# Moving the row factor of six RMS norms from the inputs of the products to their outputs, with the small vectors in three transfers and the first stage's rotation done by DVE from PSUM

## The chip, the cores and the metric

The kernel runs on one core of one Trainium2 chip. The metric is the device time of one execution, in microseconds. Engines are named as in the profile: PE multiplies matrices (PEld loads its weights), DVE is the vector engine, ACT the scalar engine, POOL is GpSimd, SP the engine that issues most transfers.

## The reference

A token block of 512 rows by 1024 columns passes through one hybrid attention layer with a gated convolution FFN and then through two more layers, each with its own attention (latent and stick-breaking heads; forgetting heads) and its own gated FFN. What matters here is the norm ahead of every projection:

```
def rms_norm(x, g):
    xf = x.astype(jnp.float32)
    y = xf * lax.rsqrt(jnp.mean(xf * xf, axis=-1, keepdims=True) + RMS_EPS)
    return (y * g.astype(jnp.float32)).astype(x.dtype)
...
    hn = rms_norm(h, attn_pre_norm)
    proj = hn @ w_in
...
    hn = rms_norm(h, ffn_pre_norm)
    u = causal_dwconv(hn @ w_up, conv_w, conv_b)
```

The factor of a row is one number per token, and the gain one number per input column. So `hn @ w` equals the row factor times `(h * g) @ w`, and the factor can be applied before or after the product. In the first stage the queries and keys that come out of `proj` are rotated (`rope`: each half of a head times a cosine, plus the other half times a signed sine).

## The kernel before, in words

The 512 rows are four tiles `t` of 128. `h` stays in SBUF. Every product is made in three matmuls (`mm3`) of high and low halves: the weights arrive by SP as slabs (`raw`), POOL splits each slab into `w_hi` and `w_lo`, and four split slabs are held at a time. The left factor is `xt_hi` and `xt_lo`, the transposed rows, also in two halves. PE waits for each slab's split (`split`) and reports its use (`slab_used`), on which POOL's next split waits.

The stages follow each other in the order in which the code is written, engine by engine, with semaphores between them: `in1` (five chunks of 512, 512, 280, 512 and 256 columns, each with four slabs), `cmp`, the attention `first`, `out1`, `up1` (11 groups of four tiles), `down1`, then `in2`, the attention `mix`, `out2`, `up2`, `down2`, and `in3`, the attention `fox`, `out3`, `up3`, `down3`. No scheduler moves anything.

Norms `n0, n3, n5, n6, n7, n8` stand ahead of `in1, up1, in2, up2, in3, up3`. A norm is a chain over four engines: ACT squares a tile's rows with a running sum (L1533), DVE makes the variance (L1992), ACT takes ln and exp (L1525, L1527), DVE refines (L1983 to L1987) and multiplies row factor and gain into a copy `xn` (L2011, which the profile shows as `tok`), PE transposes that copy with eight 128x128 transposes a tile (L930), ACT writes `xt_hi` (L1541) and DVE `xt_lo` (L2021). Only two tiles of `xn` fit. The products next to a norm therefore run by pairs of tiles, (0,1) and (2,3).

In `in1`, ACT copies a chunk's four PSUM banks into `tok` (L1853 to L1870), which frees the bank for the next chunk (`in1_copy`), DVE rotates `tok` in place in SBUF (`swapped_halves`, L2098, L2100, L2102), and PE transposes the result (L814), which waits for the rotation (`in1_tok`). These transposes stand after the third slab of the next chunk. After chunk 2, DVE adds positions to the compression blocks (`block_rows`, L2435).

The small vectors (tables, gains, biases, convolution taps) arrive by 22 transfers which ACT's queue issues after the first norm (`small_loads`, L1497). Behind them on ACT stand the sines of the position table (L1838), which wait for DVE, and behind those the first chunk's copies. In `up1` to `up3` four PSUM banks hold a group's tiles and four others the next group's; ACT and DVE read them in place, and PE waits for `up_h` of two groups before.

Of the kernel before, what the change touches and what calls it, by code (L numbers as in the profile page):

```python
# [30 lines left out]
SMALLS = 22  # L31
# [14 lines left out]
PI = 3.1415925  # L46

# [32 lines left out]
def build(nc, A, out):  # L80
# [17 lines left out]
    NORMS = ["n0", "n3", "n5", "n6", "n7", "n8"]  # L98
    RMS = [p for p in NORMS if p[0] == "n"]
    WHOLE = ("n0", "n3", "n5")  # L100
    for what in ("tp", "hi", "lo"):
        share("norm", what, [(p, 2 * NT) for p in NORMS])
    share("norm", "sq", [(p, NT if p in WHOLE else 2 * NT) for p in RMS])
    share("norm", "var", [(p, NT if p == "n0" else 2) for p in RMS])
    share("norm", "y", [(p, NT if p == "n0" else 2) for p in RMS])
    share("norm", "xn", [(p, NT) for p in RMS])
# [3 lines left out]
    share("up", "h", [(p, KF) for p in UPS], 2)  # L110
    for what in ("hi", "lo"):
        share("up", what, [(p, KF) for p in UPS])
# [21 lines left out]
    sb("align_h", [P, 96])  # L134
# [36 lines left out]
    esink = sb("esink", [P, 8])  # L171
# [12 lines left out]
    v_back = sb("v_back", [P, NT, W], F32, lay)  # L184
    lay.close()
# [29 lines left out]
    rope_c = sb("rope_c", [P, NT, HD], F32, u)  # L215
    rope_s = sb("rope_s", [P, NT, HD], F32, u)
# [3 lines left out]
    w2_sb = sb("w2_sb", [P, 2, 2, HD], F32, u)  # L220
# [52 lines left out]
    u.close()
# [13 lines left out]
    xn = tok[:, 0:2 * D].rearrange("p (s n) -> p s n", s=2)  # L287
# [80 lines left out]
    def gain_ready(e, n):  # L368
        e.wait_ge(*at(f"gain_full{n % 2}", 32 * ((n + 1) // 2 if n % 2 == 0 else n // 2) + 32 * (n % 2 == 0)))
# [447 lines left out]
    def pe_project(e, name, chunks, plan, turns, tok_waits, xt, turn, hooks=None):  # L817
# [32 lines left out]
        def input_there(t):  # L850
            e.wait_ge(*at(f"{xt}_lo", 2 * t + 2))
# [1737 lines left out]
```

## Time and profile before

| | us |
|---|---|
| median of three runs (2043.35 to 2045.88) | 2044.3 |
| the profiled execution | 2044.26 |
| its span from first to last instruction | 2042.5 |
| PE busy | 1888.7 (92%) |
| POOL busy | 1105.1 (54%) |
| DVE busy | 785.3 (38%) |
| ACT busy | 470.7 (23%) |
| mean granted clock of PE | 0.972 of full |

The busy share of PE says how much of the span its matmuls cover. The chain of work that ended last is PE for 84% of the span and DVE for 8%. What a change around PE can win lies in the rest, and in stretches where the granted clock is at its lower level. Six stretches matter: the first 192.7 us (norm `n0`, `in1`, `cmp`), and the joints of stages where the other five norms stand.

### The profile page before, as it was taken

Reading aid. Unit: us, or ns where it says so; the run is one execution under the profiler, and the core shown is the slowest. Engines: PE = TensorE matmul, PEld = TensorE weight load, DVE = VectorE, ACT = ScalarE, POOL = GpSimd, SP = SyncE. Lnnn points to the kernel's source line nnn. Section 1 sums busy time; section 2 is a strip of 40 time slices with the busy share of each in tenths; the row PEclk is TensorE's granted clock in tenths of the full one; section 3 lists DMA queues with packets and bytes.
Section 4 is the critical chain, followed back from the end, with each engine's and each line's share of the span. In section 5 each row is a group of like instructions: output and inputs, shape, how many; then the busy total and the mean of one; then the engine's idle time right before and its main releaser. Section 6 shows DMA issues by size and latency. Waiting matters only on the chain.

```text
span 2042.5 us, 28343 instructions
## 1 busy us (share of the span) xinstructions
PE 1888.7 (92%) x10604; PEld 1537.1 (75%) x10604; DVE 785.3 (38%) x1174; ACT 470.7 (23%) x1164; POOL 1105.1 (54%) x714
## 2 busy tenths in 40 slices
PE   5776889799999989997999999998998899999999
PEld 4666657688888878764888888886886588888887
DVE  3776574554342034766332122004635542221100
ACT  2112553322221013445210011002225311110100
POOL 4436324376666655441556666655662456666663
PEclk9888899999999989999999999999999999999999
DMA  4223002132333322121132333222330023233232
GB/s 129 64 62 93 12 2 73 52 114 92 102 114 96 100 75 74 56 63 42 63 93 92 103 92 96 90 93 64 93 103 22 22 83 93 92 101 95 94 102 83
DMA packets 126693, 162.63 MB, mean 80 GB/s; under 512 B 12728, under 2 KB 88456, under 8 KB 126599
## 3 DMA queue, kind: packets, MB, share of 16 engines
q1 hardware_dynamic: 121697, 160.49, 25.3%
q10 hardware_dynamic: 4902, 0.82, 0.2%
q8 instruction: 66, 1.08, 0.2%
q14 instruction: 28, 0.23, 0.0%
HBM read 158.14 MB, written 2.10 MB: 78 GB/s over the span
## 4 chain that ended last, share of the span: by engine, by line
PE 84%; DVE 8%; ACT 3%; issue 2%; DMA 1%; POOL 1%; ACTq 1%; SPq 0%; DVEq 0%; POOLq 0%
PE ps L799 24%; PE ps L800 24%; PE ps L801 24%; PE ps L1154 3%; PE ps L814 1%; PE ps L930 1%; PE ps L1127 1%; DVE p_turn L2319 1%; PE ps L1201 1%; DVE nmax L2285 1%; DVE tok L2011 1%; ACT tok L1778 1%; PE ps L1217 1%; PE ps L1231 1%; DVE rstd L1987 1%
## 5 line engine op out<-in xcount | busy, mean ns | idle before, releaser
L454 POOL TENSOR_TENSOR w_lo<-raw,w_hi 128x1024 fp32r<-128x1024 f32 (+1 forms) x256 | 615.2, 2403 | 21.4
L452 POOL TENSOR_SCALAR w_hi<-raw 128x1024 fp32r<-128x1024 f32 (+1 forms) x256 | 276.2, 1079 | 517.2 <-PE ps L801 491.4
L799 PE MATMUL ps<-xt_hi,w_hi 128*128 128x512 f32 (+1 forms) x1160 | 432.6, 373 | 7.2 <-DVE xt_lo L2021 6.5
L800 PE MATMUL ps<-xt_lo,w_hi 128*128 128x512 f32 (+1 forms) x1160 | 432.0, 372 | 0.0
L801 PE MATMUL ps<-xt_hi,w_lo 128*128 128x512 f32 (+1 forms) x1160 | 431.9, 372 | 0.0
L799 PE MATMUL ps<-w_hi,xt_hi 128*128 128x512 f32 (+3 forms) x672 | 262.2, 390 | 22.8 <-ACT tok L1860 19.8
L800 PE MATMUL ps<-w_lo,xt_hi 128*128 128x512 f32 (+3 forms) x672 | 257.5, 383 | 0.0
L801 PE MATMUL ps<-w_hi,xt_lo 128*128 128x512 f32 (+3 forms) x672 | 257.3, 383 | 0.0
L799 PEld LDWEIGHTS ps<-xt_hi,w_hi 128*128 128x128 f32 x1160 | 218.9, 189 | 47.0 <-DVE xt_lo L2021 7.5
L801 PEld LDWEIGHTS ps<-xt_hi,w_lo 128*128 128x128 f32 x1160 | 218.8, 189 | 38.7
L800 PEld LDWEIGHTS ps<-xt_lo,w_hi 128*128 128x128 f32 x1160 | 218.9, 189 | 38.2
L799 PE MATMUL ps<-w_hi,hid_hi 128*128 128x512 f32 x528 | 206.1, 390 | 0.0
L800 PE MATMUL ps<-w_lo,hid_hi 128*128 128x512 f32 x528 | 205.9, 390 | 0.0
L801 PE MATMUL ps<-w_hi,hid_lo 128*128 128x512 f32 x528 | 205.7, 390 | 0.0
L799 PEld LDWEIGHTS ps<-w_hi,xt_hi 128*128 128x128 f32 x672 | 129.6, 193 | 50.0 <-issue 24.4
L2158 DVE TENSOR_TENSOR tok<-ps,tok 128x512 f32<-128x512 f32 x44 | 30.4, 692 | 353.2 <-PE ps L801 353.2
L801 PEld LDWEIGHTS ps<-w_hi,xt_lo 128*128 128x128 f32 x672 | 129.0, 192 | 23.6
L800 PEld LDWEIGHTS ps<-w_lo,xt_hi 128*128 128x128 f32 x672 | 129.5, 193 | 21.7
L466 POOL TENSOR_SCALAR w_hi<-raw 128x1024 fp32r<-128x1024 f32 (+5 forms) x48 | 46.7, 974 | 162.5 <-PE ps L801 153.7
L801 PEld LDWEIGHTS ps<-w_hi,hid_lo 128*128 128x128 f32 x528 | 99.4, 188 | 20.8
L800 PEld LDWEIGHTS ps<-w_lo,hid_hi 128*128 128x128 f32 x528 | 99.4, 188 | 20.6
L799 PEld LDWEIGHTS ps<-w_hi,hid_hi 128*128 128x128 f32 x528 | 99.4, 188 | 20.4
(319 smaller groups left out, 2243.4 us busy)
## 6 DMA issues: line engine op xcount, KB each, us to landing
raw<-in_w_up SPq DMA_DIRECT2D x88, 256.0 KB
raw<-in_l_w_gate SPq DMA_DIRECT2D x88, 256.0 KB
raw<-in_l_w_up SPq DMA_DIRECT2D x88, 256.0 KB
raw<-in_l_w_down SPq DMA_DIRECT2D x40, 512.0 KB
raw<-in_l_w_in SPq DMA_DIRECT2D x36, 512.0 KB
raw<-in_w_down SPq DMA_DIRECT2D x20, 512.0 KB
raw<-in_l_w_o SPq DMA_DIRECT2D x16, 512.0 KB
raw<-in_w_in SPq DMA_DIRECT2D x12, 512.0 KB
```

The source lines that it names most:

```text
L452: e.tensor_scalar(w_hi[:, s, 0:width], r, 1.0, 0.0, ALU.mult, ALU.add).then_inc(split, 1)
L454: e.tensor_tensor(w_lo[:, s, 0:width], r, w_hi[:, s, 0:width].bitcast(F32), ALU.subtract).then_inc(split, 1)
L466: e.tensor_scalar(view(w_hi[:, s, :]), view(raw[:, s % 2, :]), 1.0, 0.0, ALU.mult, ALU.add).then_inc(split, 1)
L799: e.matmul(o, s_hi, m_hi, start=start, stop=False)
L800: e.matmul(o, s_hi, m_lo, start=False, stop=False)
L801: return e.matmul(o, s_lo, m_hi, start=False, stop=stop)
L814: m = e.transpose(bank(ODD[i % 4], P, t * P, w), staged(name, c)[:, t, off:off + w], ident[:, :])
L930: m = e.transpose(bank(turn_bank(name, i), P, k * P), src(t)[:, (4 * q + k) * P:(4 * q + k + 1) * P], ident[:, :])
L1127: m = e.transpose(bank(4 + y, HD, (2 * kb + x) * HD), st.prob(g, x)[r, kb * P:(kb + 1) * P], ident[r, r])
L1154: m = e.matmul(ps[x * HD:(x + 1) * HD, 6 * W + kb * P:6 * W + (kb + n) * P], value(p, x, kb), st.rooms["p_turn"][:, p % 2, x, 4 * kb:4 * k ...
L1201: e.matmul(bank(b[x], n), qp[r, q, i * P:(i + 1) * P], kk[r, k, k0 * P:(i + 1) * P], start=True, stop=False)
L2158: e.tensor_tensor(half_u[:, 2 * k + 1, :], bank((ODD, EVEN)[even][2 + k]), half_u[:, 2 * k, :], ALU.mult).then_inc(*od.done(*at(f"{name}_h ...
```

## The change

**Norms.** PE transposes `h` itself, as soon as `h` is complete. The gain of a column, which after the transpose is one number per partition, is multiplied in by ACT as the scale of the copy to `xt_hi` and by DVE in the op that makes `xt_lo`. The squares and the row factor are computed beside that. The factor is applied to the results: in `in1` it is multiplied into the rotation tables and is the scale of ACT's copies of the values; in `in2` and `in3` it is the scale of ACT's copies; in `up1` to `up3` it is turned into a row vector (`rs_rows`, by four transposes of a widened copy) and DVE multiplies every PSUM tile by it in place (`scaled`), and ACT waits for that (`up_r`) and no longer for PE.

**Order on PE.** For `n0, n6, n7, n8` the transposes go by column blocks over all four tiles (`pe_turn_columns`), the first half in the midst of the product before, the second after the first slab of the next, and the products run by slabs over all four tiles. `n3` and `n5` keep the pairs (`pe_turn_pair`), because a post norm stands ahead of them.

**The first stage.** DVE rotates queries and keys straight from PSUM (`rotated`), and PE's next chunk waits for `in1_tok`.

**Small vectors.** The host lays them out in three arrays; SP issues them in the midst of the first chunk's slabs. The position table is made during `down1`. The gain loads of the norms are gone; one transfer `g_pre` takes their place.

```diff
@@ -393,10 +393,18 @@
         for t in range(NT):
-            e.dma_start(h[:, t, :], A["x"][0, t * P:(t + 1) * P, :]).then_inc(sem(f"h_full{t}"), 16)
-        gain_load(e, 0)
+            e.dma_start(h[:, t, :], A["x"][0, t * P:(t + 1) * P, :]).then_inc(sem("h_full"), 16)
+        e.dma_start(g_pre[:, :, :], A["g_pre"]).then_inc(sem("g_full"), 16)
...
+            sp_group(e, ph["in1"].g0, slabs[:2])
+            e.dma_start(smalls[:, :], A["smalls"]).then_inc(sem("small_full"), 16)
+            e.dma_start(pos_i[:, :], A["positions"]).then_inc(sem("small_full"), 16)
+            e.dma_start(table[:, :], A["table"]).then_inc(sem("small_full"), 16)
+            sp_group(e, ph["in1"].g0, slabs[2:], first=2)
...
@@ -875,7 +901,10 @@
                 for t in range(NT):
                     if s == 0:
-                        e.wait_ge(*at(f"{name}_copy", 4 * wide(name, c) - 3 + t))
+                        if name == "in1":
+                            e.wait_ge(*at("in1_tok", 4 * c - 3 + t))
+                        else:
+                            e.wait_ge(*at(f"{name}_copy", 4 * wide(name, c) - 3 + t))
...
+    def pe_turn_pair(e, name, p):
+
+        e.wait_ge(*at({"n3": "out1_res", "n5": "down1_res"}[name], 2 * p + 2))
+        for j in range(4):
+            for x in range(2):
+                for t in range(2):
+                    k = 2 * j + x
+                    m = e.transpose(bank(BY_PAIRS[name][4 * p + j], P, (2 * x + t) * P),
+                                    h[:, 2 * p + t, k * P:(k + 1) * P], ident[:, :])
...
+    def pe_turn_columns(e, name, half):
+
+        if name == "n0":
+            e.wait_ge(*at("h_full", 64))
+        else:
+            e.wait_ge(*at({"n6": "out2_res", "n7": "down2_res", "n8": "out3_res"}[name], NT * half + NT))
+        for k in range(4 * half, 4 * half + 4):
+            for t in range(NT):
+                m = e.transpose(bank(BY_COLUMNS[name][k], P, t * P), h[:, t, k * P:(k + 1) * P], ident[:, :])
+            m.then_inc(sem(f"{name}_tp"), 1)
...
+    def act_high(e, od, name, i):
+
+        e.wait_ge(*at(f"{name}_tp", i + 1))
+        for k, T, src in turned_piece(name, i):
+            op = e.activation(xt_hi[:, k, T], src, ACT.Copy, scale=gain_of(name, k))
+        op.then_inc(*od.done(*at(f"{name}_hi", i + 1)))
...
+            for p in range(2):
+                pair = (2 * p, 2 * p + 1)
+                e.wait_ge(*at(f"{name}_sq", NT + 2 * p + 2))
...
+                        e.scalar_tensor_tensor(out=half, in0=half, scalar=rstd[:, 8 + 2 * t:9 + 2 * t],
+                                               in1=gains[:, 0, c * W:(c + 1) * W], op0=ALU.mult,
+                                               op1=ALU.mult).then_inc(*od.own())
...
@@ -2128,17 +2093,29 @@
+            def scaled(j):
+                if j == 3:
+                    e.wait_ge(slab_used, 4 * (gi + g0) + 4)
+                else:
+                    e.wait_ge(*at(f"{name}_acc", 3 * gi + (j + 1)))
+                b = bank(UP_BANKS[name][1 - even][j])
+                e.tensor_tensor(b, b, rs_rows, ALU.mult).then_inc(*od.done(*at(f"{name}_r", 4 * gi + (j + 1))))
...
+        def rotated(t, off, nh, dst, twice, done):
+
+            v = bank(EVEN[t], nh * HD, off).rearrange("p (h d) -> p h d", h=nh)
...
+            e.tensor_tensor(s.rearrange("p h (a b) -> p h a b", a=2),
+                            v.rearrange("p h (a b) -> p h a b", a=2)[:, :, ::-1, :], sn, ALU.mult).then_inc(*od.own())
+            e.wait_ge(*od.latest())
+            e.tensor_tensor(v, v, rope_c[:, t, :].unsqueeze(1).broadcast_to([P, nh, HD]), ALU.mult).then_inc(*od.own())
+            e.wait_ge(*od.latest())
...
+            e.tensor_tensor(dst, v, s, ALU.add).then_inc(*done())
```

On DVE, the program before begins with the norm of the first tile, and this stands four times (`tok` in L2011 is the normed copy, `ps` is PSUM):

```order
L1992 TENSOR_SCALAR var<-ss 128x1
L1983 TENSOR_TENSOR sq_a<-rstd 128x1
L1985 SCALAR_TENSOR_TENSOR sq_a<-sq_a,var 128x1
L1987 SCALAR_TENSOR_TENSOR rstd<-sq_a,rstd 128x1
L2011 SCALAR_TENSOR_TENSOR tok<-h,rstd,gains 128x1024
L2021 TENSOR_TENSOR xt_lo<-ps,xt_hi 128x4x128 x2
```

DVE begins the changed program with the eight low halves and one norm of four columns, and then makes what the rotation needs (`smalls` and `table` are the packed vectors, `row_scale` the row factors):

```order
L1982 SCALAR_TENSOR_TENSOR xt_lo<-ps,g_pre,xt_hi 128x512 x8
L1974 TENSOR_SCALAR var<-ss 128x4
L1999 COPY row_scale<-rstd 128x4
L2362 COPY ident_x<-ident_b 64x128
L2367 TENSOR_SCALAR smalls<-smalls 128x96
L2419 TENSOR_TENSOR table<-table,row_scale 128x256 x2
L2402 TENSOR_TENSOR scratch<-ps,table 128x512
L2405 TENSOR_TENSOR ps<-ps,table 128x512
L2413 TENSOR_TENSOR tok<-ps,scratch 128x512
```

The statistics stood ahead of the transposes and stand behind them; the rotation reads `ps` in all three ops.

On ACT, between the first norm and the first chunk's results, the program before has the rest of the small loads and the sines:

```order
L1497 DMA w_sb<-in_cmp_w 128x4x64
L1838 ACT_TABLE_LOAD
L1838 ACTIVATE m_sin<-red 128x4x16 x2
L1838 ACTIVATE m_cos<-red 128x4x16 x2
L1843 ACT_TABLE_LOAD
L1860 ACTIVATE tok<-ps 128x512 x4
L1606 ACTIVATE qp<-ps 128x512 x2
```

The changed program has at this place:

```order
L1543 ACTIVATE xt_hi<-ps,g_pre 128x512 x8
L1524 ACTIVATE dump,ss<-h 128x1024 x4
L1516 ACTIVATE sq_a<-var 128x4
L1518 ACTIVATE rstd<-sq_a 128x4
L1602 ACTIVATE qp<-ps 128x512 x2
```

Neither transfers nor sines stand there any more, nor the copies of chunk 0.

On DVE at the joint from `out2` to `up2`, before, for the last two tiles (L2064 adds the product to `h`, and L2158 is the first op of `up2`):

```order
L2064 TENSOR_TENSOR h<-ps,h 128x512 x2
L1999 TENSOR_TENSOR ss<-ss 128x2
L1992 TENSOR_SCALAR var<-ss 128x2
L1987 SCALAR_TENSOR_TENSOR rstd<-sq_a,rstd 128x2
L2011 SCALAR_TENSOR_TENSOR tok<-h,rstd,gains 128x1024 x2
L2021 TENSOR_TENSOR xt_lo<-ps,xt_hi 128x4x128 x4
L2158 TENSOR_TENSOR tok<-ps,tok 128x512 x2
```

And in the changed program, from the low halves of the first four column blocks:

```order
L1982 SCALAR_TENSOR_TENSOR xt_lo<-ps,g_pre,xt_hi 128x512 x4
L2030 TENSOR_TENSOR h<-ps,h 128x512 x4
L1990 TENSOR_TENSOR ss<-ss 128x4
L1969 SCALAR_TENSOR_TENSOR rstd<-sq_a,rstd 128x4
L1994 COPY tok<-rstd 128x512
L2144 COPY gains<-ps 128x512
L2103 TENSOR_TENSOR ps<-ps,gains 128x512 x4
L2134 TENSOR_TENSOR tok<-ps,tok 128x512 x2
```

The op over the rows of `h` between the additions and the transposes is gone, and the four scalings of PSUM (L2103) are new.

## Rows read from the trace of the kernel before

**Rows 1.** PE's waits: us in total, times, longest us.

```profile
PE ps L930 <- DVE tok L2011: 48.5, 10, 11.9
PE ps L799 <- ACT tok L1860: 19.8, 2, 12.7
```

**Rows 2.** Busy time by stretch, the first norm, `in1` and `cmp`.

```profile
core 0: us, PE busy (x) PEld busy (x) DVE busy (x) ACT busy (x) POOL busy (x), PEclk, DMA share, GB/s
0.00:22.00 22.00, 3.56 (x16) 3.19 (x17) 7.80 (x12) 7.21 (x14) 13.38 (x30) 1.00 0.62 214
22.00:54.50 32.50, 28.49 (x114) 23.11 (x112) 13.41 (x21) 6.25 (x13) 12.78 (x8) 0.89 0.30 75
54.50:67.25 12.75, 0.00 (x1) 0.03 (x1) 10.49 (x29) 2.83 (x7) 6.05 (x4) 0.60 0.28 87
67.25:94.20 26.95, 26.14 (x120) 21.26 (x121) 15.19 (x24) 5.01 (x14) 6.86 (x6) 0.94 0.15 41
94.20:118.50 24.30, 17.07 (x122) 16.29 (x121) 19.25 (x23) 4.38 (x15) 12.57 (x8) 0.86 0.27 77
118.50:141.40 22.90, 22.90 (x106) 18.72 (x104) 14.29 (x21) 1.36 (x5) 9.50 (x8) 1.00 0.20 57
141.40:171.50 30.10, 17.92 (x115) 17.76 (x115) 24.94 (x28) 6.87 (x14) 14.68 (x8) 0.77 0.24 71
171.50:192.70 21.20, 13.98 (x107) 13.21 (x105) 12.45 (x10) 2.43 (x4) 19.53 (x12) 0.84 0.35 102
```

**Rows 3.** The same view of the joints at `n3`, `n5`, `n6` and `n7`.

```profile
372.60:401.70 29.10, 17.09 (x128) 16.57 (x128) 22.12 (x33) 12.81 (x27) 6.16 (x3) 0.88 0.12 37
750.80:777.70 26.90, 17.13 (x81) 16.15 (x81) 20.26 (x29) 9.94 (x24) 9.51 (x6) 0.75 0.24 70
993.60:1047.50 53.90, 50.24 (x321) 45.89 (x320) 21.84 (x28) 11.57 (x27) 26.68 (x15) 0.97 0.22 69
1265.20:1416.40 151.20, 147.56 (x657) 121.35 (x655) 28.06 (x35) 17.05 (x37) 85.33 (x60) 0.99 0.25 77
```

**Rows 4.** The start: landing of `h`, last split of chunk 0, DVE's wait for loads.

```profile
DMA to landing us min/median/max: 3.4/5.1/6.8
...
24.79 2.38 POOL L468 TENSOR_TENSOR w_lo<-raw,w_hi 128x1024 fp32r<-128x1024 f32 x1
...
51.10 0.15 DVE L2379 TENSOR_SCALAR g_col<-g_col 128x1 f32<-128x1 f32 x1 [13.19 <-DMA w_sb<-in_cmp_w]
```

**Rows 5.** Eight transposes, start us and us, at either clock.

```profile
20.38 1.97 PE L930 MATMUL ps<-ident,tok 128*128 128x128 f32 x8 [6.52 <-DVE tok L2011]
...
1033.35 1.03 PE L930 MATMUL ps<-ident,tok 128*128 128x128 f32 x8
```

**Rows 6.** One line's instructions: ns min/median/max, first and last start us.

```profile
L2158 DVE TENSOR_TENSOR tok<-ps,tok x44: 690/692/692, 1047.1 to 1918.6; 128x512 f32<-128x512 f32 x44
L2100 DVE TENSOR_TENSOR tok<-tok,rope_c x24: 291/692/2711, 77.4 to 180.1; 128x256 f32<-128x256 f32 x12, 128x512 f32<-128x512 f32 x8, 128x128 f32<-128x128 f32 x4
```

**Rows 7.** DVE's `block_rows` between chunks 3 and 4 of `in1`.

```profile
136.59 10.22 DVE L2435 TENSOR_TENSOR gains<-kvc,pe_t 64x248 f32<-64x248 f32 x16
```

**Rows 8.** The joint at `n3`: additions to `h`, first transposes.

```profile
371.37 5.28 DVE L2265 SCALAR_TENSOR_TENSOR h<-mixed,rstd,h 128x1024 f32<-128x1024 f32 x2
...
381.31 3.56 PE L930 MATMUL ps<-ident,tok 128*128 128x128 f32 x16 [8.71 <-DVE tok L2011]
```

**Rows 9.** The joint at `n5`, both pairs of tiles.

```profile
744.95 1.41 DVE L2055 SCALAR_TENSOR_TENSOR scratch<-ps,rstd,gains 128x512 f32<-128x512 f32 x2
...
762.03 0.69 DVE L2021 TENSOR_TENSOR xt_lo<-ps,xt_hi 128x512 fp32r<-128x512 f32 x1 [0.16 <-ACT xt_hi L1541]
...
769.19 1.23 DVE L2059 TENSOR_TENSOR h<-h,scratch 128x1024 f32<-128x1024 f32 x1
...
757.58 3.78 PE L930 MATMUL ps<-ident,tok 128*128 128x128 f32 x16 [6.79 <-DVE tok L2011]
```

**Rows 10.** Busy time in the middle of `up1`.

```profile
411.00:620.00 209.00, 209.00 (x933) 173.47 (x932) 97.26 (x120) 53.99 (x80) 141.73 (x79) 1.00 0.34 104
```

More of the change, by code:

```diff
@@ L30 @@
 CMP, CMPS = 32, 16
-SMALLS = 22
 NCB = SEQ // CMPS - 1
@@ L110, in build @@
     share("up", "h", [(p, KF) for p in UPS], 2)
+    share("up", "r", [(p, 44) for p in UPS])
+    for what in ("wide", "bt", "bc"):
+        share("up", what, [(p, 1) for p in UPS])
     for what in ("hi", "lo"):
@@ new lines, in pe_out_direct @@
+    def pe_out_direct(e, name, there, norm):
+        for c in range(2):
+            for s in range(4):
+                e.wait_ge(split, 2 * (4 * (phases[name].g0 + c) + s) + 2)
+                if c == 0:
+                    e.wait_ge(*there[s])
+                for t in range(NT):
+                    m = slab_tile(e, name, c, s, OUT_KTS[s], x_model, KD - 1, t)
+                m.then_inc(slab_used, 1)
+                if c == 1 and s == 1:
+                    pe_turn_columns(e, norm, 0)
@@ L1466, in decays @@
                 for x in range(t + 1):
-                    m = e.matmul(bank(7, 16, t * 16), (tri if x == t else ones)[:, :], logf[:, x, :],
+                    m = e.matmul(bank(LOW[3], 16, t * 16), (tri if x == t else ones)[:, :], logf[:, x, :],
                                  start=x == 0, stop=x == t)
@@ L1521, in act_rstd @@
+        pe_out_direct(e, "out3", [at("fox_lo", 2 * s + 2) for s in range(4)], "n8")
+        pe_up(e, "up3", "n8")
+        pe_down(e, "down3", "up3", None)
     def act_rstd(e, od, name, k, n, a=0, step=1):
@@ L1950, in put @@
                     rows = tok3[:, t, :].rearrange("p (h d) -> p h d", d=HD)
-                    e.activation(rows, bank(EVEN[t]).rearrange("p (h d) -> p h d", d=HD), ACT.Copy).then_inc(
+                    e.activation(rows, bank(HIGH[t]).rearrange("p (h d) -> p h d", d=HD), ACT.Copy, scale=rs[:, t:t + 1]).then_inc(
                         *od.done(cp, last))
@@ L1954, in put @@
                 else:
-                    e.activation(v3[:, t, (c - 5) * W:(c - 4) * W], bank(EVEN[t]), ACT.Copy).then_inc(*od.done(cp, last))
+                    e.activation(v3[:, t, (c - 5) * W:(c - 4) * W], bank(HIGH[t]), ACT.Copy,
+                                 scale=rs[:, t:t + 1]).then_inc(*od.done(cp, last))
             return put
@@ L2149, in chunk @@
             else:
+                for j in range(4):
+                    scaled(j)
                 for k in range(2):
@@ L2387, in _ @@
+        hooks, variance = dve_cat()
+        dve_pair_attend(e, od, first, hooks)
+        for r, q in (HALVES, HALVES[::-1]):
+            e.tensor_copy(strict_x[r, :], strict[q, :]).then_inc(*od.own())
+        dve_out1(e, od, variance)
+        dve_up(e, od, "up1", True)
+        e.wait_ge(slab_used, 4 * phases["down1"].g0)
         e.tensor_copy(pos_f[:, :], pos_i[:, :]).then_inc(*od.own())
@@ L2474, in _ @@
-        hooks, variance = dve_cat()
-        dve_pair_attend(e, od, first, hooks)
-        for r, q in (HALVES, HALVES[::-1]):
-            e.tensor_copy(strict_x[r, :], strict[q, :]).then_inc(*od.own())
-        dve_out1(e, od, variance)
-        dve_up(e, od, "up1", True)
-        dve_out(e, od, "down1", 4, "n5", 5)
+        dve_out(e, od, "down1", "n5")
         plan = t_plan(T_IN2)
```

891 lines of the change are left out of this document (430 added, 461 removed).

## The prediction

> **What bounds the kernel now.** The busy shares come first: PE is busy for 1888.7 us of the 2042.5 us span, so at most some 154 us can come from filling PE, and a little more from stretches in which its clock is at the lower level. The list of waits says for what PE stood still [rows 1]: 48.5 us in ten waits for the normed copy of a tile (L2011), and 19.8 us in two waits for ACT's copies (L1860), one of them 12.7 us. The change touches the makers of both. The table of stretches says where [rows 2]: in the first 192.7 us, PE is busy for 130 us. At 0 to 22 us it waits for `n0`, at 54.5 to 67.25 us it does nothing at all, and chunks 2 and 4 (from 94.2 and 141.4 us) hold 7.2 and 12.2 us without work. Chunk 3, from 118.5 us, shows what a chunk costs undisturbed: 22.9 us at a clock of 1.00, with 96 matmuls and 8 transposes. The transposes take 1.03 us [rows 5], so a matmul of 512 columns takes (22.9 - 1.0)/96 = 0.228 us. Last I read the joints [rows 3]: PE is busy 17 of 29 us at `n3`, 17 of 27 at `n5`, 50 of 54 at `n6`. The middle of `up1` is the contrast [rows 10]: PE is busy for all of 209 us, ten groups of 20.9 us, and DVE for 9.7 us of each.
>
> **The first stage, step by step.** The last issue of `h` is at about 2 us, and the landing takes at most 6.8 us [rows 4]: 9.0 us. PE then turns all of `h`, 32 transposes, at the low clock of a cold start 1.97/8 = 0.246 us each [rows 5]: 7.9 us, to 16.9. DVE's and ACT's halves follow by column block. The last split of chunk 0 was done at 27.2 us [rows 4], before PE comes to it. Chunk 0 takes 96 x 0.228 = 21.9 us and 1.3 us for the slow start: it ends at 40.0, where it ended at 54.5.
>
> Then came the 12.75 us gap [rows 2]. Its cause is a queue: ACT's copies of chunk 0 stood behind sines, these behind DVE's angles, and these behind the wait for the 22 small loads, which DVE leaves at 51.1 us after 13.2 us [rows 4]. In the new order neither loads, sines nor copies stand there. DVE must have the factors and the scaled tables. It gets the squares at about 25 us, then small ops of 2.5 us, two copies of identities (I allow 4.8 us, since POOL is busy beside them) and two scalings of the table: 33 to 37 us, before 40. So the gap goes, and what remains is the exchange of banks. A tile of the rotation is three ops of 512 columns. That DVE reads and writes PSUM in place in `tensor_tensor` stands in no row; L2158, with one input in PSUM, takes 0.69 [rows 6], and two operations in SBUF of the same width are the other bound, up to 2.71. I take 0.69 because the new ops have at most one input in SBUF, like L2158. With the waits between them a tile takes 2.25 us, against PE's 1.36 us for a tile of the next chunk (6 matmuls): a stall of about 1 us an edge.
>
> Chunk 1: 21.9 + 2.0 of transposes + 1 of edge + 1.5 in reserve = 26.3, ending at 66.3 instead of 94.2. Chunk 2 (280 columns): 12.2 of matmuls + 2.8 of edge + 4.7 of transposes at half clock = 19.7, to 86.0 instead of 118.5; its 7.2 us of idle time were waits for rotations in SBUF, which L2100 shows at up to 2.71 us where its least is 0.29 [rows 6], and L2158 never above 0.692 though POOL is busy for half of the span. Chunk 3: 22.9, to 108.9. Chunk 4: `block_rows` with its 10.2 us on DVE [rows 7] stays ahead of the rotation of chunk 3, and now PE's first matmul waits for that rotation as well: 31 us instead of 30.1, since a wait of some 10.3 us opens it but the 5 us in its midst shrink; to 139.9. `cmp`: bound by the arrival and splitting of its weights (POOL busy 19.5 of 21.2 us [rows 2]), 20.7 us, to 160.6 instead of 192.7. **Gain 32.1 us.** If the 5 us are no longer there to shrink, or the reserve is used twice, it is 26 to 29; if POOL slows the tables too, PE waits from 40 on, us for us.
>
> The trace ties the long forms of L2100 to operations with both inputs in SBUF [rows 6]. The Trainium skill, "SBUF — State Buffer", section "SBUF: two separate sides", says why: such a DVE operation and a GpSimd operation lock one pair of ports against each other, for a whole instruction. By that rule, which the trace bears out, the rotation from PSUM is free of POOL. A rule against the change is in "VectorE: DVE Perf Modes", section "The TRN2 errata": 120 fixed cycles for a PSUM source, 58 for SBUF, some 65 ns an operation; over the 36 added ones of `in1` that would be an estimate of 2.4 us, and 1984 for the whole. L2158 at 692 ns from PSUM shows a 512-column op that leaves no room for much of it.
>
> **The joints.** `n3`: `h` is ready at 376.65 and the transposes start at 381.31 after 8.7 us of idling [rows 8]; between lies L2011. Starting at 376.7 saves 4.6, and 1.5 more as low halves go out by column block and the first slab takes them one by one; the row vector costs PE four transposes, 0.5, and I keep 0.4 for a late `up_bc`: **5.2 us**. `n5`: `h` of the first pair needs, from 744.95 [rows 9], four ops of 0.70, two of 1.23 and 0.7 of waits: 751.0, so its transposes start 6.6 us before 757.58, and their last low half comes at 755.9. The second pair's `h` came 7.7 us behind that (762.72 to 770.42 [rows 9]): 763.6. Transposes of 3.8 and 0.9 to the first low half make 768.3 for the second pair's products, where they began at 777.7, the end of the stretch [rows 3]. That is 9.4, less 1.4 for a low clock (0.75 in the stretch) that I don't expect to go: **8.0 us**. `n6`: now 53.9 us [rows 3]. New: 96 matmuls of `out2` at 0.228, 96 of `up2` at full width, where 192 half-wide ones stood, at 20.9/96 = 0.218 [rows 10], 32 transposes at 4.1, the row vector 0.5, and 0.6 in reserve: 48.0. The cover is the matmul work between additions and transposes: half of the column blocks wait for nothing while two slabs still run, the other half are issued a slab later. `n8` has the same form: **5.9 us twice**. `n7`: 624 matmuls at 0.227 and 4.2 of transposes are 145.8, against 151.2 [rows 3]: **5.4 us**. If a joint's cover is gone it pays the statistics again, 2 to 4 us each.
>
> **What is added in `up1` to `up3`.** Four scalings of a PSUM tile by a vector in SBUF per group. No row shows it; L2158 at 0.69 is the nearest, the SBUF form of up to 2.71 the upper bound [rows 6]. Four times 0.69 is 2.8: DVE goes from 9.7 to 12.5 us of 20.9 [rows 10]. At the upper bound it is 20.5, and just hidden. ACT now waits for DVE instead of PE, but PE needs a bank only two groups on. I cost it at nothing; if the cover went, every us above 20.9 is paid in each of 33 groups. ACT's scale and DVE's gain in the halves cost nothing of their own (0.69 and 0.70 for the same widths).
>
> **Sum.** 32.1 + 5.2 + 8.0 + 11.8 + 5.4 = 62.5 us. The profiled execution took 2044.26 us, as the median of 2044.3: 2044.3 - 62.5 = 1981.8, say **1982**.
>
> **Rivals.**
> *Half of the start.* Speaks for it: the edges of five chunks go through DVE now, and the factors need squares, variance, copies and a table in a row, all with POOL's building of constants beside them (POOL busy 13.4 of the first 22 us [rows 2]). A table ready at 50 instead of 37 keeps 10 us; four edges at 2 to 3 us more keep 6 to 12. Against it: PSUM ops aren't slowed in any row. Time: 1982 + 16 = 1998.
> *Half of the joints.* PE may meet the next thing late: in `n6` to `n8` the column block's halves, in `n3` and `n5` the post norm's additions, which the change leaves alone; and a clock that has fallen (0.75 at `n5`) may stay down. Time: 1982 + 15 = 1997.
> *Slower.* The scalings decide: ACT reads only after `scaled`, DVE needs ACT's result for the rest of the group, so a group may become a chain. It costs more than the rest wins once a group takes 20.9 + 62.5/33 = 22.8 us; at 24 us the time is 1982 + 33 x 3.1 = 2084. Against it: 8.4 us of DVE free per group and two sets of banks.
> *No gain.* The transposes wait for something else as late, at the start the constants or the last tile of `h`, at the joints the additions: about 2044.
> *More.* Over 75 us, if the clock stays at 1.00 through start and joints and chunk 4 loses its wait: 1965.
>
> **How the numbers follow.** Forecast 0.66, with a range of its own of 1970 to 1995 (2.25 us or 3 us a rotated tile, table at 33 or 42, joints 1 to 2 us each either way); half of the start 0.15; half of the joints 0.08; more 0.06; slower 0.03; no gain 0.02. 1970 to 2004 takes in the first three but for their far edges, and a part of "more": over 8 in 10. A measurement of this kernel tells 0.2%, 4 us, from no change; faster by more holds every case but the last two: 0.95, 0.02 the same, 0.03 slower.
>
> **What would show it.** Right: PE's first transposes at about 9 us; chunk 0 over at 40; no wait of PE above 3 us before chunk 2; no wait for ACT's `tok` at chunk 1; chunk 4 opened by a wait of some 10 us; `cmp` over at 161; transposes of `n3` and `n5` right behind L2265 and L2059; at `n6`, `n7`, `n8` PE busy without a gap; L2103 132 times near 0.69, DVE busier by some 90 us, PE's busy time about as before. Wrong: a rotated tile well above 2.25 us, the scaled table after 42 us, PE waits before the second pair of `n5` above 4 us, PE busy below 100% in the midst of `up1`, or a lower granted clock there.

## The result, and the profile after

| | us |
|---|---|
| before, median of four runs | 2045.1 |
| changed, median of four runs (2006.7 to 2016.0) | 2012.0 |
| ratio, 95% interval | 0.9836 (0.9806 to 0.9866) |
| forecast | 1982, range 1970 to 2004 |

The change makes the kernel 33 us faster, half of what was forecast, and the time lies 8 us above the range. The profiled execution took 2015.36 us, with a span of 2013.2 us.

The list of PE's waits is the first thing to read, beside [rows 1]:

```profile
PE ps L1160 <- DVE p_turn L2298: 24.3, 31, 3.6
PE ps L814 <- DVE tok L2413: 12.8, 7, 9.8
PE ps L962 <- DMA h<-in_x: 9.2, 1, 9.2
PE ps L814 <- POOL w_lo L457: 8.0, 4, 2.4
...
PE ps L950 <- DVE h L2020: 4.4, 1, 4.4
...
PE ps L950 <- DVE h L2247: 4.0, 1, 4.0
...
PE ps L814 <- ACT dump L1884: 2.3, 1, 2.3
```

The 48.5 us of waits for the normed copy and the 19.8 us for ACT's `tok` are gone. In their place stand 9.2 us for `h` at the start, 9.8 us at the head of chunk 4, and 4.0 and 4.4 us at `n3` and `n5` (L2247 and L2020 are the additions to `h`, L2265 and L2059 in the kernel before). (The first line is in attention and was there before.) Next the first stage, in windows cut at PE's chunk edges, beside [rows 2]:

```profile
0.00:9.25 9.25, 0.00 (x1) 0.03 (x1) 0.00 (x0) 1.28 (x1) 3.94 (x23) 1.00 0.76 270
9.25:14.55 5.30, 5.30 (x33) 5.29 (x33) 3.11 (x5) 3.68 (x6) 3.77 (x3) 1.00 0.74 285
14.55:36.90 22.35, 22.35 (x98) 18.16 (x97) 17.48 (x27) 6.40 (x13) 21.10 (x12) 1.00 0.49 141
36.90:61.90 25.00, 24.61 (x113) 19.63 (x112) 9.27 (x21) 3.07 (x8) 9.64 (x9) 1.00 0.24 68
61.90:78.90 17.00, 15.53 (x121) 15.06 (x120) 7.37 (x22) 4.03 (x11) 12.34 (x8) 1.00 0.33 94
78.90:102.20 23.30, 23.30 (x106) 18.73 (x104) 10.08 (x21) 1.21 (x4) 9.18 (x8) 1.00 0.24 68
102.20:112.00 9.80, 0.04 (x1) 0.00 (x0) 9.61 (x14) 1.99 (x2) 2.07 (x2) 0.65 0.16 54
112.00:131.00 19.00, 17.78 (x112) 16.93 (x113) 8.64 (x16) 2.30 (x5) 10.21 (x6) 0.73 0.19 56
131.00:152.20 21.20, 13.23 (x108) 12.03 (x106) 3.08 (x9) 2.25 (x3) 18.20 (x13) 1.00 0.42 128
```

The first stage ends at 152.2 us instead of 192.7, 40 us earlier. That alone is more than the 33 us of the whole. So something after it costs time that no wait shows. PE's busy time says the same: it has risen from 1888.7 to 1911.2 us, with fewer instructions (10,416 for 10,604). The place to look is a stretch in which nothing was changed and PE never rests, `down1`: 528 matmuls of 512 columns, busy to 100% at a clock of 1.00. Before:

```profile
630.95:750.79 119.84, 119.84 (x529) 98.91 (x527) 13.16 (x20) 10.25 (x23) 71.91 (x45) 1.00 0.28 86
```

And after, with a stretch of `up2` behind it:

```profile
593.03:715.88 122.85, 122.85 (x531) 99.58 (x530) 27.43 (x49) 13.05 (x27) 72.03 (x46) 1.00 0.29 87
999.83:1229.67 229.84, 229.84 (x988) 184.96 (x987) 67.73 (x84) 25.51 (x42) 141.72 (x82) 1.00 0.30 94
```

The same work takes 122.85 us for 119.84. The pitch, the time from the start of one matmul to the start of the next, is on average 232.4 ns in this `down1` against 226.7 ns before, and 233.3 ns in the stretch of `up2`. It is no wait and no clock: on average a matmul of 512 columns starts 5.7 to 6.6 ns later after the one before it. The delay isn't even. Before, the starts stand 226 or 227 ns apart; in the changed kernel's `up2` 229 and 237 or 238 ns in turn.

### The profile page after: what moved, and what is told of

It is laid out like the page before. It is cut to its first block, busy times and chain, and to the rows that moved or that the text cites. A ratio compares the mean times of both kernels' runs of the same rounds, so it can differ in the third digit from the quotient of the medians.

```text
span 2013.2 us, 28099 instructions
## 1 busy us (share of the span) xinstructions
PE 1911.2 (95%) x10416; PEld 1519.0 (75%) x10416; DVE 797.1 (40%) x1283; ACT 470.6 (23%) x1144; POOL 1081.5 (54%) x713
## 3 DMA queue, kind: packets, MB, share of 16 engines
q1 hardware_dynamic: 121409, 158.21, 25.6%
## 4 chain that ended last, share of the span: by engine, by line
PE 86%; DVE 7%; ACT 4%; issue 1%; POOL 1%; DMA 1%; SPq 0%; DVEq 0%; POOLq 0%; ACTq 0%
PE ps L814 25%; PE ps L815 25%; PE ps L816 25%; PE ps L1187 3%; PE ps L1160 1%; PE ps L829 1%; DVE p_turn L2298 1%; DVE nmax L2264 1%; PE ps L1234 1%; ACT dump L1524 1%; ACT tok L1764 1%; PE ps L962 1%; ACT xt_hi L1543 1%; PE ps L1264 1%; PE ps L1250 1%
## 5 line engine op out<-in xcount | busy, mean ns | idle before, releaser
L457 POOL TENSOR_TENSOR w_lo<-raw,w_hi 128x1024 fp32r<-128x1024 f32 (+1 forms) x256 | 606.5, 2369 | 21.3
L455 POOL TENSOR_SCALAR w_hi<-raw 128x1024 fp32r<-128x1024 f32 (+1 forms) x256 | 267.5, 1045 | 551.1 <-PE ps L816 515.6
L814 PE MATMUL ps<-xt_hi,w_hi 128*128 128x512 f32 (+2 forms) x1096 | 427.1, 390 | 0.9 <-ACT tok L1932 0.9
L815 PE MATMUL ps<-xt_lo,w_hi 128*128 128x512 f32 (+2 forms) x1096 | 426.3, 389 | 0.0
L816 PE MATMUL ps<-xt_hi,w_lo 128*128 128x512 f32 (+2 forms) x1096 | 426.2, 389 | 0.0
L2103 DVE TENSOR_TENSOR ps<-ps,gains 128x512 f32<-128x512 f32 x132 | 92.1, 698 | 395.3 <-PE ps L816 395.3
L814 PEld LDWEIGHTS ps<-xt_hi,w_hi 128*128 128x128 f32 (+1 forms) x1096 | 206.0, 188 | 48.7 <-POOL w_lo L471 1.3
L815 PEld LDWEIGHTS ps<-xt_lo,w_hi 128*128 128x128 f32 (+1 forms) x1096 | 205.9, 188 | 47.5
L816 PEld LDWEIGHTS ps<-xt_hi,w_lo 128*128 128x128 f32 (+1 forms) x1096 | 205.8, 188 | 47.6
L2030 DVE TENSOR_TENSOR h<-ps,h 128x512 f32<-128x512 f32 x32 | 22.1, 691 | 261.4 <-PE ps L816 261.3
```

What stands on the lines that cost most here:

```text
L455: e.tensor_scalar(w_hi[:, s, 0:width], r, 1.0, 0.0, ALU.mult, ALU.add).then_inc(split, 1)
L457: e.tensor_tensor(w_lo[:, s, 0:width], r, w_hi[:, s, 0:width].bitcast(F32), ALU.subtract).then_inc(split, 1)
L814: e.matmul(o, s_hi, m_hi, start=start, stop=False)
L815: e.matmul(o, s_hi, m_lo, start=False, stop=False)
L816: return e.matmul(o, s_lo, m_hi, start=False, stop=stop)
L2030: e.tensor_tensor(h[:, t, cs], out_half(name, c, t), h[:, t, cs], ALU.add).then_inc(*od.done(*at(f"{name}_res", NT * c + t + 1)))
```

## The experiments

**Where the pitch of the matmuls comes from.** One thing in the change touches all stages: the layout of SBUF. The diff ahead of the prediction left these lines out:

```diff
-    sb("align_h", [P, 96])
     h = sb("h", [P, NT, D])
     raw = sb("raw", [P, 2, SLAB])
     w_hi = sb("w_hi", [P, 4, SLAB], F32R)
     w_lo = sb("w_lo", [P, 4, SLAB], F32R)
...
+    sb("align_x", [P, ALIGN])
```

`ALIGN` is 12. With the first pad gone, `h`, `raw`, `w_hi` and `w_lo` start 384 bytes lower (`w_hi` at byte 41088 of each partition instead of 41472). The new pad keeps `xt_hi`, `xt_lo`, `hid_hi` and `hid_lo` exactly where they were (`xt_hi` at 106240). The first four runs were made together.

`e1_buffers_back` is the changed kernel with

```diff
+    causal = sb("causal", [P, P], BF16)
+    ss = sb("ss", [P, 32])
     h = sb("h", [P, NT, D])
```

> The changed kernel, with two small buffers (causal and ss, 384 bytes a partition together) declared ahead of h, so that h, raw, w_hi and w_lo stand at the addresses that they had before the change; nothing else differs. Theory A (the address of the weight buffers sets the pitch of the matmuls, 226.8 ns before and 232.5 after): the pitch goes back to 226.8 ns in every stage and the time falls by 5.6 ns for each of some 6,900 matmuls of 512 columns, about 38 us, to 1972 to 1978. Theory B (DVE's scalings in PSUM, or the changed program as such, slow PE): no change, 2005 to 2016, pitch 232.

Measured: 1982.6 us (1979.1 to 1985.2), 0.9693 (0.9677 to 0.9710) of before, 29 us below the changed kernel. `down1` and the same piece of `up2` in its trace:

```profile
587.42:707.26 119.84, 119.84 (x530) 99.00 (x528) 28.41 (x49) 13.05 (x27) 72.21 (x46) 1.00 0.28 88
991.12:1214.46 223.34, 223.34 (x988) 185.04 (x987) 67.68 (x84) 25.55 (x42) 141.49 (x82) 1.00 0.31 97
```

119.84 us again, and starts 226.7 ns apart in both. Theory A holds; the time is 5 us above its range, on which more below.

`e2_before_moved` is the kernel before with only this:

```diff
-    sb("align_h", [P, 96])
     h = sb("h", [P, NT, D])
...
     scratch = sb("scratch", [P, 2, W])
+    sb("align_h", [P, 96])
     ident = sb("ident", [P, P])
```

> The kernel before, with its leading pad of 384 bytes moved behind scratch, so that h, raw, w_hi and w_lo stand where the changed kernel has them; nothing else differs. Theory A: pitch 232 instead of 226.8 ns, and 2045 + 38 = 2083 us. Theory B: 2045, pitch 226.8.

Measured: 2083.3 us (2081.0 to 2085.5), 1.019 (1.0173 to 1.0207) of before: 38.4 us for a pad that no instruction reads. By the starts in the two traces, its 6,191 matmuls of 512 columns come 5.7 ns later each (232.6 for 226.9 ns on average), which is 35 us of it. Its `down1`:

```profile
642.26:765.12 122.86, 122.86 (x529) 99.38 (x527) 13.18 (x20) 10.45 (x23) 71.94 (x45) 1.00 0.28 84
```

`e3_scaling_one_column` tests the rival that DVE's new traffic in PSUM slows PE:

```diff
-                e.tensor_tensor(b, b, rs_rows, ALU.mult).then_inc(*od.done(*at(f"{name}_r", 4 * gi + (j + 1))))
+                e.tensor_tensor(b[:, 0:1], b[:, 0:1], rs_rows[:, 0:1], ALU.mult).then_inc(*od.done(*at(f"{name}_r", 4 * gi + (j + 1))))
```

> The changed kernel with each of the 132 scalings in up1 to up3 cut to one of its 512 columns, so the row factor of the other columns is left out there. Theory A: DVE's busy time falls by some 83 us, the pitch stays at 232, and the time stays within 0.2% of 2012. Theory B in its first form (DVE's traffic in PSUM slows PE): the pitch in up1 to up3 falls to 227 and the time by about 3168 x 5.6 ns = 18 us, to 1994.

Measured: 2014.0 us (2012.3 to 2018.1), no change. DVE's busy time fell from 797.1 to 721.7 us and PE's stayed (1910.9 for 1911.2). The scalings are free, and the rival falls. The trace of the changed kernel says the same of every other engine: in the stretch of `up2` the mean pitch is 233.2 ns under matmuls with POOL busy throughout and 233.4 ns with POOL idle, 233.4 and 233.3 ns with DVE busy and idle. So it isn't traffic of another engine that delays the matmuls.

The next four, run once beside their profile, ask which address counts. They are the changed kernel with `causal` and `ss` between `raw` and `w_hi` (e5), with `ALIGN = 44` (e6), with `ss` alone ahead of `h` (e7), and with `causal` alone ahead of `h` (e8).

> The changed kernel with causal and ss (384 bytes) declared between raw and w_hi: the split weights stand where they stood before the change, h and raw stay at their changed addresses. If the weights' address is what counts: pitch 226.8 ns and 1980 to 1985, as e1. If it is that of h or raw: 232 ns and 2012.

> The changed kernel with ALIGN 44 in place of 12, so that xt_hi, xt_lo, hid_hi and hid_lo move up by 128 bytes; the weights stay where the change put them. Addresses modulo 256: weights 128 and left factors 128, where the changed kernel has 128 and 0, and the kernel before 0 and 0. If the pitch hangs on the two operands having the same remainder: 226.8 ns and about 1982. If each operand off a multiple of 256 costs by itself: 232 or more, 2012 or more.

> The changed kernel with ss alone ahead of h: h, raw and the weights move up by 128 bytes, weights at 41216 (modulo 256: 0, modulo 512: 256). If a multiple of 256 is enough: 226.8 ns and about 1982. If it takes 512: 232 ns and 2012.

> The changed kernel with causal alone ahead of h: everything up to scratch moves up by 256 bytes, weights at 41344 (modulo 256: 128, modulo 512: 384). Theory of a modulus of 256: as the changed kernel, 232 ns and 2012. If any shift of the layout helps: less.

The table has the start addresses modulo 256 of the weights' buffers and of the left factor's buffers, the matmuls that the windows count from 1720 to 1860 us (PE is busy for all 140 us, at a clock of 1.00), and the time. (e2, with 128 and 0, is left out: it does narrower matmuls in part of that window.)

| kernel | weights | left factor | matmuls in 140 us | us |
|---|---|---|---|---|
| before | 0 | 0 | 619 | 2045.1 |
| changed | 128 | 0 | 601 | 2012.0 |
| e3 | 128 | 0 | 602 | 2014.0 |
| e8_shift_256 | 128 | 0 | 602 | 2008.3 |
| e1 | 0 | 0 | 620 | 1982.6 |
| e5_only_weights_back | 0 | 0 | 619 | 1983.8 |
| e7_shift_128 | 0 | 0 | 619 | 1984.0 |
| e6_left_factor_128 | 128 | 128 | 620 | 1979.7 |

One row of e6 and one of e8:

```profile
1720.00:1860.00 140.00, 140.00 (x620) 115.91 (x619) 45.07 (x55) 18.05 (x29) 88.36 (x52) 1.00 0.31 97
```

```profile
1720.00:1860.00 140.00, 140.00 (x602) 112.63 (x601) 43.81 (x54) 15.86 (x26) 86.51 (x50) 1.00 0.30 94
```

`h` and `raw` don't matter (e5), a remainder by 512 neither (e7). e6 decides between two forms of the theory: both operands off a multiple of 256 by the same 128 bytes run at the fast pitch. What counts here is that the addresses of the two operands of a matmul leave the same remainder modulo 256. Only the remainders 0 and 128 were tried. Why the difference costs time, no run shows.

**What holds back the first stage.** `e4_rows_later` is e1 with

```diff
-            if c == 2:
+            if c == 3:
                 block_rows()
                 block_rows_low()
```

> As e1_buffers_back, and block_rows (10 us on DVE) stands behind the rotation of chunk 3 instead of ahead of it. If the 9.8 us wait that opens chunk 4 is the price of that order alone, the wait shrinks to about 1 us and the time falls by 6 to 9 us against e1. The rival: cmp is bound by POOL's splits of its weights (four PE waits of 1.8 to 2.4 us there now), or by the block rows that then come later, and takes most of it back: less than 3 us.

Measured: 1983.1 us (1972.0 to 1985.2), as e1. PE's waits from 95 to 160 us:

```profile
PE ps L814 <- DVE f_lo L2390: 12.4, 1, 12.4
PE ps L814 <- POOL w_lo L457: 4.0, 2, 2.1
PE ps L814 <- DVE tok L2413: 1.9, 2, 1.1
```

The wait of 9.9 us has left the head of chunk 4 and stands as 12.4 us at the head of `cmp`, which needs those rows. The rival with "block rows that then come later" was right: the last matmul of `cmp` ends at 154.5 us for 154.3. (One of e4's four executions took 1972.0 us, at a mean granted clock of 0.985; the others took 1981.2 to 1985.2 us at 0.977 to 0.980. Four executions can't tell a few us.)

`e11_rows_in_two_parts` is e1 with

```diff
             if c == 2:
-                block_rows()
-                block_rows_low()
+                block_rows((0,))
+            if c == 3:
+                block_rows_low((0,))
+                block_rows((1,))
+                block_rows_low((1,))
```

> As e1_buffers_back, but block_rows is cut in two: the keys' half (5 us on DVE) ahead of the rotation of chunk 3, the values' half behind it. The order of e4 moved the wait of 9.8 us from the head of chunk 4 to the head of cmp, 12.5 us. If both waits are the price of 10 us of DVE work in one piece, the two halves cost about 4.5 us at chunk 4 and 0 to 4 at cmp: cmp ends 3 to 6 us earlier than in e1 (154.3), 1976 to 1980. Rival: cmp is bound by the arrival and splitting of its slabs, which follows PE: less than 2 us.

Measured: 1982.4 us (1975.8 to 1984.6), no difference from e1. The same list:

```profile
PE ps L829 <- DVE tok L2413: 14.7, 1, 14.7
PE ps L814 <- DVE tok L2413: 4.2, 4, 2.3
PE ps L814 <- POOL w_lo L457: 0.9, 1, 0.9
```

Now it stands before the transposes of chunk 4, whose rotation is queued behind the second half. `cmp` was expected to end 3 to 6 us earlier than in e1 and ends at 155.8 us, 1.5 later. POOL's splits, the rival of my text for e11, cost next to nothing (0.9 us). By these waits the bound of the stretch is DVE's chain, wherever PE meets it; no run makes that chain shorter.

`e9_rotate_through_sbuf` is e1 with

```diff
-            e.tensor_tensor(v, v, rope_c[:, t, :].unsqueeze(1).broadcast_to([P, nh, HD]), ALU.mult).then_inc(*od.own())
+            y = gains[:, 1, off:off + nh * HD].rearrange("p (h d) -> p h d", h=nh)
+            e.tensor_tensor(y, v, rope_c[:, t, :].unsqueeze(1).broadcast_to([P, nh, HD]), ALU.mult).then_inc(*od.own())
             e.wait_ge(*od.latest())
+            v = y
```

> As e1_buffers_back, but the rotation of the first stage writes its cosine product to a buffer in SBUF instead of back to PSUM, so that the last of its three operations has both inputs in SBUF. Theory (the rotation from PSUM is what keeps it clear of POOL): the last operation, 0.69 us in e1, takes up to 2.7 us wherever POOL works, the exchange of banks costs PE some 1 to 2 us more per chunk in chunks 1 to 4, and cmp ends 4 to 8 us later than in e1 (154.3), so 1986 to 1991. Rival: the length of a rotated tile doesn't matter there, since PE waits for other things: within 2 us of e1, 1982.

Measured: 1980.8 us (1973.1 to 1986.1), as e1; `cmp` ends at 155.5 us. The last operation of the rotation does grow, as expected, but seldom:

```profile
L2415 DVE TENSOR_TENSOR tok<-gains,scratch x24: 291/692/1981, 37.3 to 139.5; 128x256 f32<-128x256 f32 x12, 128x512 f32<-128x512 f32 x8, 128x128 f32<-128x128 f32 x4
```

PE's waits for the rotation from 30 to 160 us are 17.1 us, for 14.8 in e1. By the two traces the price is about 2 us and not 4 to 8, too small for these runs to tell.

`e10_small_loads_late` is e1 with the three packed loads moved behind two slabs of chunk 1.

> As e1_buffers_back, but the three packed loads are issued in the midst of chunk 1's slabs instead of chunk 0's. My step was that the 12.75 us gap after chunk 0 was the queue of small loads: the slabs of chunk 1 are issued only as the raw buffers come free, up to about 40 us, so the scaled table would be late by some 5 to 8 us, PE would wait that long behind chunk 0 where it waits 1.5 us in e1, and the time would be 1987 to 1992. Rival: the loads land before DVE asks for them either way: 1982.

Measured: 1979.7 us (1973.4 to 1981.5), no slower. The loads are issued 21 us later and DVE doesn't notice. (Its first stage even ends at 150.3 us, since the wait behind chunk 0 is missing; that is the luck of one split, as said at the end of the next section.) Its timeline:

```profile
28.52 0.98 DVE L2363 COPY causal_x<-causal 64x128 bf16<-64x128 bf16 x1
29.53 0.19 DVE L2362 COPY strict_x<-band 64x128 bf16<-64x128 bf16 x1
...
32.31 0.74 DVE L2419 TENSOR_TENSOR table<-table,row_scale 128x256 f32<-128x256 f32 x2
```

SP issues them from 25.1 to 26.6 us, and DVE needs none before 32. My text took the `raw` buffers for occupied until 40 us, which is wrong. So the early place of the loads is not needed. What the gap of 12.75 us was made of, the queue of 22 loads, the sines or the copies behind them, the runs did not take apart.

**A version that beats both.** `e12_combined` is e11 with the identity copies and the scaling of three small vectors moved behind the rotation of chunk 0, and this in ACT's post norms:

```diff
                 act_rstd(e, od, name, p + 1, 2, 8 + 4 * p, 2)
+                if p:
+                    act_norm(e, od, norm, (0, 1), False)
                 for j in range(4):
                     act_high(e, od, norm, 4 * p + j)
-            act_norm(e, od, norm)
+            act_norm(e, od, norm, (2, 3))
```

> As e11, and two more moves: DVE makes the identity copies and scales three small vectors behind the rotation of chunk 0 instead of ahead of the table (some 5 us of operations that POOL lengthens), and ACT squares the first two tiles of n3 and n5 in the time in which it waits for the second pair, 2.4 us earlier. Expected against e11: the 1.5 us wait behind chunk 0 gone, and the 2.4 us wait of PE in in2 shrunk to 0.3: 2 to 4 us less, 1973 to 1977. Rival: the clock gives it back, or DVE's small operations of n5 stay locked out by POOL: no difference from e11.

Measured: 1969.7 us (1964.9 to 1976.0), 0.9635 (0.9604 to 0.9665) of before: 75 us below before, 42 below the changed kernel and 13 below e11, more than expected, though the slowest of its executions and the fastest of e11 (1976.0 and 1975.8) just meet. The two profiled executions are 10.0 us apart: 4.6 us in the first stage (`cmp` ends at 151.2 us for 155.8) and 4.7 us behind `down1`. The wait in `in2` is gone, and behind chunk 0 PE waits 0.3 us for 2.1. From the end of `down1` to the value products of the second attention it takes 146.7 us for 151.4 in e11, and the granted clock of that stretch is 0.99 for 0.97. The wait ahead of chunk 4's transposes stays (15.0 us).

## Why the prediction was wrong

Most of its mechanisms held and its range did not, because of a term that it didn't have.

**The step that failed** is "PE's busy time about as before", and with it every product in which I carried a pitch of the old trace into the new kernel (0.228, 0.227, 0.218 us a matmul). The pitch is no constant of the shape. It rose by 2.5 to 2.9% with the layout of SBUF. By e2 that is 38.4 us; between e1 and the changed kernel it is 29.4 us. The lines that decide it stood in the full diff, and I didn't weigh them. With the buffers back, e1 takes 1982.6 us where 1982 was forecast. Part of that agreement is luck, as the terms show.

The terms, by the span from a mark to the next in the traces of before and e1:

| term | forecast | e1 against before |
|---|---|---|
| first stage | 32.1 | 38.4 |
| `n3` | 5.2 | 5.1 |
| `n5` | 8.0 | 2.2 |
| `n6`, `n8` | 11.8 | 6.4 + 6.5 |
| `n7` | 5.4 | 5.9 |
| second and third attention | 0 | -1.3, -1.0 |
| sum | 62.5 | 62.2 |

The term of `n5` goes to the end of `in2`. No run takes the changed terms one by one: the table says in which stretch the time went, not by which edit.

**The first stage** was under-estimated by 6 us. The step "at the low clock of a cold start" was wrong for half of the 32 transposes: PE turned `h` in 5.3 us, not 7.9.

```profile
9.25 5.50 PE L962 MATMUL ps<-ident,h 128*128 128x128 f32 x32 [9.25 <-DMA h<-in_x]
14.55 0.47 PE L814 MATMUL ps<-w_hi,xt_hi 128*128 128x512 f32 x1
14.86 0.39 PE L815 MATMUL ps<-w_lo,xt_hi 128*128 128x512 f32 x1
15.09 0.39 PE L816 MATMUL ps<-w_hi,xt_lo 128*128 128x512 f32 x1
```

By their starts, the transposes go at 213 ns until 12.9 us and at 109 ns from there, and chunk 0 has the full pace from its second matmul on. In the kernel before, with its pauses, the first matmuls of chunk 0 still started every 427 ns from 22.6 to 25.6 us. So chunk 0 was over at about 37 us, not 40. The larger miss is chunk 2, costed at 19.7 us with 4.7 us of "transposes at half clock": it took 17.0 us in the changed kernel and in e1, at a granted clock of 1.00. In e1 the stage is 6.3 us shorter than forecast, of which 1.3 us stand ahead of chunk 1, 0.6 in chunk 1, 2.7 in chunk 2 and 1.8 in chunk 4. The wait for chunk 3's rotation was forecast at 10.3 us and is 9.8. The table was ready in time in the changed kernel, at 33.5 us. A rotated tile takes 2.07 us for the 2.25 taken, by DVE's timeline:

```profile
33.56 0.69 DVE L2402 TENSOR_TENSOR scratch<-ps,table 128x512 f32<-128x512 f32 x1
34.28 0.70 DVE L2405 TENSOR_TENSOR ps<-ps,table 128x512 f32<-128x512 f32 x1
35.02 0.69 DVE L2413 TENSOR_TENSOR tok<-ps,scratch 128x512 f32<-128x512 f32 x1
35.63 0.68 DVE L2402 TENSOR_TENSOR scratch<-ps,table 128x512 f32<-128x512 f32 x1
```

So `tensor_tensor` in place in PSUM costs 0.70 us, as bounded. The Trainium skill's "VectorE: DVE Perf Modes", section "The TRN2 errata", has 120 fixed cycles for a PSUM source and 58 for SBUF, by my estimate 65 ns an operation; between 0.70 us in place in PSUM and the 0.69 us of the last operation with both inputs in SBUF (at 42.35 us in e9) no such difference appears. The 20.7 us for `cmp` were right (21.2). The reason that I gave for the gap after chunk 2, lengthened operations in SBUF, is only partly tested: e9 brings one of the three operations back to two inputs in SBUF and finds some 2 us in all chunks together. The other two weren't tried.

**`n5`** was mis-sized by 5.8 us. The products of the second pair start as forecast: from the end of `down1` to them are 17.2 us in the changed kernel, 9.7 less than before [rows 3]. But I counted nearly the whole of that as gain. Twelve matmuls of the first pair (2.3 us) were done before that mark in the old order and come behind it in the new one. A chunk later PE waits 2.3 us, because ACT can't copy before the row factor is there, and from 735 to 745 us of e1, in the midst of which that wait lies, the granted clock is 0.83, where it was 1.00 in the same work before: some 1.7 us more, by my estimate. The wait of 4.4 us for the second pair's additions lies inside the 17.2 us; it was one of the signs of being wrong ("above 4 us"). The row factor is late by DVE's timeline of the changed kernel:

```profile
739.70 1.97 DVE L1965 TENSOR_TENSOR sq_a<-rstd 128x4 f32<-128x4 f32 x1 [0.51 <-ACT rstd L1518]
741.71 0.97 DVE L1967 SCALAR_TENSOR_TENSOR sq_a<-sq_a,var 128x4 f32<-128x4 f32 x1
742.71 0.17 DVE L1969 SCALAR_TENSOR_TENSOR rstd<-sq_a,rstd 128x4 f32<-128x4 f32 x1
742.91 2.26 DVE L1997 TENSOR_SCALAR row_scale<-rstd 128x4 f32<-128x4 f32 x1
745.08 0.16 DVE L1998 TENSOR_SCALAR row_scale<-rstd 128x4 f32<-128x4 f32 x1
```

And POOL beside it:

```profile
739.24 2.41 POOL L471 TENSOR_TENSOR w_lo<-raw,w_hi 128x1024 fp32r<-128x1024 f32 x1
741.62 1.05 POOL L469 TENSOR_SCALAR w_hi<-raw 128x1024 fp32r<-128x1024 f32 x1
742.75 2.39 POOL L471 TENSOR_TENSOR w_lo<-raw,w_hi 128x1024 fp32r<-128x1024 f32 x1
```

Each of DVE's three long operations ends when POOL's does (741.67 and 741.65, 742.68 and 742.67, 745.17 and 745.14 us). An operation on four columns takes 0.16 us or, caught by one of POOL's splits, 1 to 2.3. The Trainium skill's rule in "SBUF — State Buffer", section "SBUF: two separate sides", agrees in that one engine waits out a whole instruction of the other; here it is small operations that pay. In e12 the last squares come 2.3 us earlier, and the factor stands 23 us after the end of `down1` instead of 29, partly since fewer of these operations were caught (one of 1.03 us there); the wait is gone.

**`n6`, `n7`, `n8`** came out as forecast and 0.5 us better each: PE is busy without a gap there in the changed kernel (50.70 of 50.70 us at `n6`). The 0.218 us for a full-width matmul of `up` was a slip: 209 us hold more than nine but not ten groups, so it is 0.227, and a group is 21.8 us. With it the forecast for `n6` and `n8` would have been 5.0 us each, and the measured gain is 1.4 us above that. **The scalings** cost nothing, as said; L2103 stands 132 times at 699 ns, and e3 shows it. But DVE isn't "busier by some 90 us": it went from 785.3 to 797.1 us, since the 92.1 us of scalings replace, among others, the normed copies (L2011, 39.4 us).

**The rivals.** "Half of the start" and "half of the joints" didn't happen (the first stage gave more than all of its term). "Slower" didn't either. The time came out near the worse cases for a reason that was in none of them.

**Why e1 stood 5 us above its own range.** I expected 38 us back and got 29. The pitch did what it should: 6,383 matmuls of 512 columns, 6.1 ns faster on average (226.9 for 233.0), are 39 us. But some stretches gained nothing by it. The first stage ends at 154.3 us in e1 and at 152.2 in the changed kernel, and from the end of `down1` to the end of `in2` both take 130 us.

For part of the first stage the traces show the reason, and it is chance. Behind chunk 0, PE waits 2.2 us for the first rotated tile in e1 and 0.4 in the changed kernel. It isn't that faster matmuls reach the wait sooner: e3, with the slow pitch, has chunk 1 start at 38.6 us as e1 does (38.7), and e6, with the fast pitch, at 36.6 as the changed kernel does (36.9). What differs is whether a split by POOL catches the scaling of the tables. First the changed kernel, then e1 with POOL's split:

```profile
32.78 0.75 DVE L2419 TENSOR_TENSOR table<-table,row_scale 128x256 f32<-128x256 f32 x2
```

```profile
33.38 2.95 DVE L2419 TENSOR_TENSOR table<-table,row_scale 128x256 f32<-128x256 f32 x2
33.49 2.56 POOL L471 TENSOR_TENSOR w_lo<-raw,w_hi 128x1024 fp32r<-128x1024 f32 x1
```

In e1 the granted clock is 0.85 from 40 to 50 us, behind this wait. The mean clock of the profiled span is 0.978 in e1 and 0.983 in the changed kernel. That a wait draws the lower clock after it fits here, but I made no run that separates the two, and what kept `in2` at 130 us stays open.

## What to carry to other kernels

Where a change moves the layout of buffers, compare the pitch of matmuls in an untouched, fully busy stretch before reading any wait; a term "as before" is a claim about addresses too. Give both operands of a matmul the same remainder modulo 256 (0 or 128 here), and put a pad there on purpose. When a wait has moved twice and the end has not (e4, e11), it is the chain behind it that has to become shorter. When a chain of small DVE operations runs beside POOL's splits, compare several traces before giving a wait of 2 us a cause. And when a joint is costed, end the stretch at a mark with the same work behind it in both kernels.

## What the runs showed of the hardware that was not expected

Matmuls of 512 columns in float32r, back to back at a clock of 1.00, start every 226.7 ns when the start addresses of stationary and moving operand agree modulo 256, and every 232.4 to 233.3 ns on average when they differ by 128. No wait and no clock shows it, and the busy share is 100% either way. At the start of the program PE goes at half pace (transposes every 213 ns) in both kernels, while the granted clock of these stretches reads 1.00. The traces hold no record of the clock ahead of 13.0 us (26.2 us in the kernel before), and that is where the pace doubles: the column doesn't show this phase. A DVE operation over four columns in SBUF took up to 2.3 us beside POOL's work, and 0.16 us alone.
